# Contracting the meta tokens' values over 128 partitions instead of 16 in a stick-breaking attention step

## What is computed

```python
z = einsum('bqhd,bkhd->bhqk', q, k) * HD ** -0.5
a = where(mask, exp(log_sigmoid(z) + suffix), 0.0)   # suffix: sum of log(1 - beta) over later keys
o = einsum('bhqk,bkhd->bqhd', a, v)                  # keys are 16 meta tokens, then the prompt
y_s = silu(z_s) * o
```

## Time and profile before

| | |
|---|---|
| median of 3 runs | 1778.04 us (1777.66 to 1778.42) |
| profiled execution, its own time | 1776.47 us |
| its span, first to last instruction | 1774.7 us |
| PE busy | 1734.5 us, 98% of the span |
| PEld busy | 1619.1 us, 91% |
| DVE, ACT, POOL busy | 565.3, 512.5, 364.3 us |
| mean granted clock | 0.991 |

### The profile page before, as it was taken

One profiled execution on the slowest core, in us unless ns is written; L12 is line 12 of the kernel. 1 busy time (PEld: TensorE's weight loads), 2 busy tenths in 40 slices (PEclk: granted clock), 3 DMA queues, 4 the chain that ended last, 5 costly groups with the idle time before them and its releaser, 6 DMA issues.

```text
span 1774.7 us, 28110 instructions
## 1 busy us (share of the span) xinstructions
PE 1734.5 (98%) x10469; PEld 1619.1 (91%) x10469; DVE 565.3 (32%) x920; ACT 512.5 (29%) x1225; POOL 364.3 (21%) x326
## 2 busy tenths in 40 slices
PE   8999999999999999999999999999999999799998
PEld 7999999998999999988888888888888887599998
DVE  5333332333000000024344343434343433545211
ACT  6211122211111111224343333424243433512111
POOL 3111221212112121322131212112121210412111
PEclk9999999999999999999999999999999999899999
DMA  4111111111121221333232322323232122543244
GB/s 158 48 36 35 47 47 36 39 43 36 64 75 65 72 86 63 108 89 99 74 107 65 98 64 82 92 78 107 66 109 63 59 63 71 165 143 121 84 124 122
DMA packets 227899, 142.23 MB, mean 80 GB/s; under 512 B 8151, under 2 KB 220711, under 8 KB 227805
## 3 DMA queue, kind: packets, MB, share of 16 engines
q1 hardware_dynamic: 227804, 140.94, 26.7%
HBM read 112.98 MB, written 27.93 MB: 79 GB/s over the span
## 4 chain that ended last, share of the span: by engine, by line
PE 95%; DMA 2%; issue 1%; ACT 1%; SPq 1%; DVE 0%; POOL 0%; DVEq 0%; ACTq 0%; POOLq 0%
PE bank_p L75 21%; PE bank_p L76 21%; PE bank_p L77 21%; PE bank_o L1112 6%; PE bank_z L1054 4%; PE bank_o L76 3%; PE bank_o L77 3%; PE bank_o L75 3%; PE bank_t L1101 2%; PE bank_s L1081 2%; PE bank_s L1126 2%; PE bank_t L1067 2%; DMA wqkv_raw<-y_s_scratch 1%; PE bank_z L76 1%; PE bank_z L77 1%
## 5 line engine op out<-in xcount | busy, mean ns | idle before, releaser
L75 PE MATMUL bank_p<-x_hi,w_hi 128*128 128x384 f32 (+1 forms) x1024 | 349.9, 342 | 5.0 <-ACTq L559 4.3
L77 PE MATMUL bank_p<-x_hi,w_lo 128*128 128x384 f32 (+1 forms) x1024 | 347.6, 339 | 0.0
L76 PE MATMUL bank_p<-x_lo,w_hi 128*128 128x384 f32 (+1 forms) x1024 | 347.5, 339 | 0.0
L158 POOL TENSOR_TENSOR w_lo<-w_raw,w_hi 128x1024 fp32r<-128x1024 f32 x56 | 139.5, 2490 | 557.0 <-ACT w_hi L153 557.0
L75 PE MATMUL bank_p<-wqkv_hi,x_hi 128*128 128x384 f32 (+1 forms) x640 | 218.9, 342 | 2.7 <-DVE v_rows L1363 2.7
L77 PE MATMUL bank_p<-wqkv_hi,x_lo 128*128 128x384 f32 (+1 forms) x640 | 212.2, 332 | 0.0
L76 PE MATMUL bank_p<-wqkv_lo,x_hi 128*128 128x384 f32 (+1 forms) x640 | 212.1, 331 | 0.0
L75 PEld LDWEIGHTS bank_p<-x_hi,w_hi 128*128 128x128 f32 x1024 | 193.1, 189 | 7.2 <-POOL w_lo L158 4.6
L77 PEld LDWEIGHTS bank_p<-x_hi,w_lo 128*128 128x128 f32 x1024 | 193.0, 189 | 0.0
L76 PEld LDWEIGHTS bank_p<-x_lo,w_hi 128*128 128x128 f32 x1024 | 192.9, 188 | 0.0
L1380 DVE TENSOR_TENSOR_SCAN one_minus_beta<-one_minus_beta 128x1040 f32<-128x1040 f32 (+8 forms) x72 | 108.0, 1500 | 63.8 <-ACT one_minus_beta L1224 63.8
(11 more groups left out here) (212 smaller groups left out, 3014.2 us busy)
## 6 DMA issues: line engine op xcount, KB each, us to landing
w_raw<-in_w_in SPq DMA_DIRECT2D x48, 512.0 KB, 3.8
cache_k_rows<-in_cache_k SPq DMA_DIRECT2D x64, 256.0 KB, 3.0
cache_v_rows<-in_cache_v SPq DMA_DIRECT2D x64, 256.0 KB, 3.3
wqkv_raw<-in_w_in SPq DMA_DIRECT2D x24, 512.0 KB, 5.3
m_part_scratch<-gates_out SPq DMA_DIRECT2D x8, 576.0 KB, 2.8
gate_scratch<-gates_out SPq DMA_DIRECT2D x8, 576.0 KB, 2.8
gate_s<-gate_scratch SPq DMA_DIRECT2D x8, 576.0 KB, 3.9
m_part<-m_part_scratch SPq DMA_DIRECT2D x8, 576.0 KB, 5.0
```

What stands on the lines that cost most here:

```text
L75: pe.matmul(out, lh(k), rh(k), start=k == 0, stop=False)
L76: pe.matmul(out, lh(k), rl(k), start=False, stop=False)
L77: mm = pe.matmul(out, ll(k), rh(k), start=False, stop=k == KC - 1)
L158: pool.tensor_tensor(self.lo[:, s, :, :], self.raw[:, s, :, :], self.hi[:, s, :, :].bitcast(F32), ALU.subtract).then_inc(self.lo_ok, 1)
```

## The change

The meta item's product contracts over all 128 partitions. Its turned weights go into a buffer of their own, `atm` (a_meta_turned), of which only partitions 0 to 15 are ever written by ACT; POOL sets the whole of it to zero once, and the META_TILE of `v` too. To make room, the scratch tile of the squares (`junk`) moves into an area that was left empty.

```diff
@@ gpsimd, before the first head
         pool.memset(half[:, :], -0.5).then_inc(half_ok, 1)
+        pool.memset(atm[:, :, :], 0.0).then_inc(half_ok, 1)
+        pool.memset(v[:, :, META_TILE, :], 0.0).then_inc(half_ok, 1)
         pool.memset(qbd[:, :], 0.0).then_inc(half_ok, 1)
         pool.memset(ats[:, :, :, :], 0.0).then_inc(half_ok, 1)
-        pool.wait_ge(half_ok, 3)
+        pool.wait_ge(half_ok, 5)
@@ tensor, weigh
                 t = META_TILE if item == "meta" else item
-                n = rows_of(t)
-                mm = pe.matmul(c.bank_o[:, 0:P], v[0:n, par, t, :], at[0:n, gg % 2, m * P:(m + 1) * P],
+                a_t = atm[:, prompt_units_before(u) % 2, :] if item == "meta" else at[:, gg % 2, m * P:(m + 1) * P]
+                mm = pe.matmul(c.bank_o[:, 0:P], v[:, par, t, :], a_t,
@@ scalar, copy_a
-                act.activation(at[0:META, gg % 2, 0:P], bank[0:META, 0:P], ACT.Copy)
+                act.activation(atm[0:META, prompt_units_before(u) % 2, :], bank[0:META, 0:P], ACT.Copy)
@@ late_buffers
-        c.sb(ctx, "room_above_gates", [P, 3 * P])
+        b.junk = c.sb(ctx, "squares2", [P, 2, P])
+        c.sb(ctx, "room_above_gates", [P, P])
...
-            b.junk = c.sb(rest, "squares2", [P, 2, P])
...
+            b.atm = c.sb(rest, "a_meta_turned", [P, 2, P])
```

More of the change, by code:

```diff
@@ L776, in attention @@
     beta, keep, at, ats, kc, vc, kt = buf.beta, buf.keep, buf.at, buf.ats, buf.kc, buf.vc, buf.kt
+    atm = buf.atm
     qbd, ot, zs, atn, orow = buf.qbd, buf.ot, buf.zs, buf.atn, buf.orow
```

## The result

The changed kernel takes **1753.36 us** (median of 4 runs, 1749.58 to 1757.34) against 1777.85 us for the kernel before (4 runs, 1775.93 to 1778.42): a ratio of 0.9866 with a 95% interval of 0.9843 to 0.9888, some 24 us less. Forecast were 1755.0 us and a range of 1751.5 to 1759.0. The profiled executions are 20.9 us apart: 1776.47 before, 1755.55 after, which is 2 us above the 1753.5 that the sum gave for it.

What follows compares the result with a forecast made beforehand. PE was taken to bound the attention, so its savings move the end one to one. 21.3 + 1.7 - 0 = 23.0 us off 1776.47 gave 1753.5, or 1755.0 us on the median's scale; range 1751.5 to 1759.0.

Steps and rivals of the forecast that it cites:

- term 1: Meta product on 128 rows in heads 0 to 6: 56 products at 0.38 us each, 21.3 us off PE.
- term 2: The last head's eight meta products: 1.7 us saved, bounds 1.1 and 3, only where PE stands in the chain.
- terms 3 and 4: ACT's copy to another tile and moved scratch: 0; two POOL memsets, some 0.6 us, covered by 3.7 us: 0.
- term 5: Weights or cache values late when PE reaches each slot 0.38 us earlier: nearest margin 0.9 us, so nothing takes its place.
- The start of the unit as the cause: Rival: the gap belongs to a unit's first product, not its rows; time stays at 1778.0 us; chance 0.04.
- A wait in the place of the stop: Rival: PE comes early, cache values or a copy are late; 10.7 us come back, 1765.7 us; chance 0.04.
- The clock: Rival: more active array rows make the granted clock in 815 to 1490 us leave 1.00; 1796 us; chance 0.02.
- The rule that a load overlaps only with another row group: Full-row products would expose every weight load, padding gains nothing, time stays at 1778.0 us; shares a rival's 0.04 chance.

Runs made afterwards that it cites:

- with the turn too: The changed kernel with the turn of the meta tokens' keys, once a head, also on 128 rows; against the kernel before: 1753.90 us, ratio 0.9855.

## Why the prediction was right, and where it was off

*The meta product (term 1).* 21.3 us were forecast for heads 0 to 6, and 7 x 3.10 = 21.7 us is what heads without a disturbance give. The mechanism is shown from three sides: the stop moves with the product and not with the start of the unit, it is paid per change and not per product, and it is gone at 96 and 128 rows and whole at 16 and 64. The text put it at "about 0.19 us each time", and that is half of 0.387. That the weight load does not lie beside the running matmul at such a change is read from the loads' starts; what holds it back no run shows.

*The last head (term 2).* This step failed by its size. It was put at 1.7 us with bounds of 1.1 and 3, and the profiled executions show about 0.4 in its first unit and -0.1 from there to the merge, -0.1 + 0.4 = 0.3. Three more profiles of kernels without the stop show 1.0 (the changed kernel again), 0.7 (96 rows) and 0.35 us (with the turn too) from the first take-out to the merge, so 1.4, 1.1 and 0.7 with the first unit. What was read rightly is that a saving counts there only up to the first transfer: the third unit's take-out stood 0.74 us nearer to the first's than before, and nothing was gained in the fourth unit. The seventh gave 0.3 where 0.2 was put. The eighth gave 0.28 where 0.4 was put: the four full-row passes were priced at 0.214 us, the spacing inside a dense row, but the pass that starts after a wait is followed more slowly, and all four take 1.02 us and not 0.86. What the term left out is that the stretch behind the savings does not stay as it was: 0.70 us more for the samples' products at the lower clock level and 0.54 for a transfer took the gain away. Those vary from one execution to the next by more than the 0.6 us that were counted on; the last of the transfers took 3.80 to 5.65 us in the four profiles without the stop.

*ACT's copy, the scratch and the memsets (terms 3 and 4).* Nothing, as forecast: two memsets of 0.31 us, covered to the last hundredth at 746.62, and an unchanged head with everything in place but the rows.

*What could be late next (term 5).* Nothing was, in heads 0 to 6. In the last head, where the transfers are dense, PE waited once for the cache values, 0.4 us.

*The rivals.* The start of the unit as the cause: ruled out by weighing the meta item last. A wait in the place of the stop: no new wait in heads 0 to 6. The clock: the granted clock from 815 to 1470 us has a mean of 0.99, with the loss at the loop's turns and not behind the products. (The text there calls three quarters of the array's rows unused; with 16 of 128 in use it is seven eighths. Nothing hangs on it.) The rule that a load overlaps only with another row group, which the prediction takes from the Trainium skill (page "TensorE: Matmul & The Clock Gate", Part 3), falls with the first: loads of full-row products, which share all row groups, go on 0.112 us apart behind the meta product too.

*What the sum left out.* The turns of the loop and the short losses of clock move single executions by 2 us each, and they hid the difference of the two profiles from the sum more than any term did. The range allowed for it. The 1.6 us at the start of the last head were in no term either. All four profiles without the stop have them against the kernel before. If the other executions do too, they make up for what the last head gave less, and the medians, 24.5 us apart where 23.0 were forecast, came that close partly by luck. The heads' 21.7 us were read, not luck.

## What to carry to other kernels

Where small products on few partitions stand among full ones, look at the distance between starts at their edges: if PE stands there, padding the contraction with zeros is cheaper than the narrow product, since the passes cost the same and only the stops go. Pad far enough: here 96 rows served as well as 128, and 64 gained nothing. It takes a zeroed tile for each of the two operands, of which nothing but the real rows is ever written again, and a place for the memsets where another engine covers them. Where padding can't be had, put narrow products next to one another, so that they share one stop in and one out.

## What the runs showed of the hardware that was not expected

- The cost does not shrink with the rows left unused. 16 and 64 rows cost 0.38 to 0.39 us a product, 96 rows nothing. The Trainium skill lists row configurations of 128, 64 and 32 rows and says that changing the mode "drains the TensorE" (page "TensorEngine Tiling (Array Packing)", Available Configurations and Key Properties). This trace agrees in so far as PE stands for about 0.19 us at each change beside full-row products; that 96 rows run in the same mode as 128 is inferred from their costing nothing.
- Going from 16 rows directly to products on 32 columns costs one stop, not two (0.2 us less, twice a head).
- Few columns do not stop PE everywhere. The products on 32 columns do (0.99 us instead of 0.90 for the eight passes ahead of them, above). The turn of the meta weights does not: it uses 16 columns ("128\*16") and stands in one row with full turns; after the change it and six of them take from 928.72 to 929.41, 0.10 us each:

```profile
928.72 0.93 PE L1104 MATMUL bank_t<-ident,beta 128*16 128x128 f32 x7
929.41 0.42 PE L75 MATMUL bank_p<-wqkv_hi,x_hi 128*128 128x384 f32 x1
```

- The turn of the loop costs PE about 2 us (1.94 to 2.45) on "issue", and whether the clock falls behind it differs between executions.
